# Two edits in a diffusion backbone kernel: feed-forward products added to the residual by GpSimd's transfers, and values' two parts in one stationary block

## The reference

```python
n = rmsnorm(h, norm_g[l, 0]) * (1 + sc0) + s0
h = h + 0.5 * g0 * swiglu(n, w_ffn_up[l, 0], w_ffn_down[l, 0])      # feed-forward, width 2816
n = rmsnorm(h, norm_g[l, 1]) * (1 + sc1) + s1
y, ckv, k_r = token_mix(n, ...)       # long convolution, 8-head attention, Fourier mixing, gates
h = h + g1 * y
n = rmsnorm(h, norm_g[l, 2]) * (1 + sc2) + s2
h = h + 0.5 * g2 * swiglu(n, w_ffn_up[l, 1], w_ffn_down[l, 1])
# in token_mix, per head of value width 64:
p = softmax(q @ k.T * scale);  o = p @ v
```

## Time and profile before

| | us |
|---|---|
| median of 3 runs | 3137.64 |
| the profiled execution's own time | 3137.54 |
| its span in the trace | 3135.4 |
| PE busy | 3018.9 (96%) |
| DVE busy | 2122.9 (68%) |
| ACT busy | 1141.8 (36%) |
| POOL busy | 85.8 (3%) |

### The profile page before, as it was taken

How to read it: one execution, slowest core, us unless ns; L and a number is a source line. 1 busy time by engine, 2 the same in 40 slices (tenths; PEclk the granted TensorE clock), 3 DMA queues, 4 the chain that set the end, 5 groups by cost and what they waited for, 6 DMA issues and landing times.

```text
span 3135.4 us, 48664 instructions
## 1 busy us (share of the span) xinstructions
PE 3018.9 (96%) x19892; PEld 2938.2 (94%) x19892; DVE 2122.9 (68%) x3521; ACT 1141.8 (36%) x1820; POOL 85.8 (3%) x164
## 2 busy tenths in 40 slices
PE   7999999998999999999999999999899999999998
PEld 4899999997899999999999999999789999999998
DVE  7666666646655557988968988863565556785675
ACT  3422312422444433434343433442154443443432
POOL 0000000000000000000000000000000000000000
PEclk8999999999999999999999999999999999999999
DMA  8255553345122532444322434334521242122222
GB/s 304 91 202 228 213 190 135 115 153 221 67 75 85 192 112 80 135 141 142 122 95 94 149 121 142 108 114 163 224 82 71 76 186 108 68 95 81 95 68 75
DMA packets 89743, 408.90 MB, mean 130 GB/s; under 512 B 10049, under 2 KB 13569, under 8 KB 68914
## 3 DMA queue, kind: packets, MB, share of 16 engines
q1 hardware_dynamic: 60384, 285.76, 25.6%
q0 software_dynamic: 19872, 94.53, 8.3%
q10 hardware_dynamic: 9266, 25.50, 2.2%
HBM read 359.46 MB, written 46.30 MB: 129 GB/s over the span
## 4 chain that ended last, share of the span: by engine, by line
PE 77%; DVE 14%; ACT 4%; issue 3%; DMA 1%; ACTq 0%; DVEq 0%
PE tile_psum L743 21%; PE misc_psum L860 12%; PE tile_psum L750 11%; PE misc_psum L864 6%; PE tile_psum L1215 6%; PE tile_psum L704 3%; PE tile_psum L1219 3%; PE misc_psum L669 3%; PE tile_psum L669 2%; PE tile_psum L860 2%; PE tile_psum L709 2%; PE tile_psum L1080 1%; DVE h L2254 1%; DVE wlo L2083 1%; PE tile_psum L864 1%
## 5 line engine op out<-in xcount | busy, mean ns | idle before, releaser
L743 PE MATMUL tile_psum<-n_hi,whi 128*128 128x320 f32 x1536 | 352.3, 311 | 4.0 <-issue 2.2
L743 PE MATMUL tile_psum<-n_lo,whi 128*128 128x320 f32 x1536 | 350.1, 309 | 0.0
L2083 DVE TENSOR_TENSOR wlo<-raw,whi 128x2048 fp32r<-128x2048 f32 (+4 forms) x130 | 250.6, 1930 | 114.2 <-ACT whi L1491 112.2
L743 PE MATMUL tile_psum<-x_hi,whi 128*128 128x320 f32 x1300 | 300.1, 312 | 17.4 <-DVE h L2254 11.7
L743 PE MATMUL tile_psum<-x_lo,whi 128*128 128x320 f32 x1300 | 298.3, 311 | 0.0
L743 PEld LDWEIGHTS tile_psum<-n_hi,whi 128*128 128x128 f32 x1536 | 257.6, 189 | 6.8 <-DVE n_lo L2174 4.2
L743 PEld LDWEIGHTS tile_psum<-n_lo,whi 128*128 128x128 f32 x1536 | 258.2, 189 | 0.0
L1491 ACT ACTIVATE whi<-raw 128x2048 fp32r<-128x2048 f32 (+4 forms) x130 | 208.9, 1616 | 126.7 <-DMA raw<-in_w_down 43.7
L1215 PE MATMUL tile_psum<-n_hi,whi 128*128 128x320 f32 x768 | 237.4, 320 | 11.0 <-ACT gate_out L1978 10.3
L2254 DVE SCALAR_TENSOR_TENSOR h<-tile_psum,ada_t,h 128x320 f32<-128x320 f32 (+2 forms) x408 | 154.2, 434 | 129.2 <-PE tile_psum L750 127.5
L750 PE MATMUL tile_psum<-n_hi,wlo 128*128 128x320 f32 x1536 | 241.3, 309 | 0.0
(11 more groups left out here) (384 smaller groups left out, 6450.1 us busy)
## 6 DMA issues: line engine op xcount, KB each, us to landing
w_ada<-in_w_ada POOLq DMA_DIRECT2D x72, 512.0 KB, 4.0
raw<-in_w_up SPq DMA_DIRECT2D x72, 512.0 KB, 3.8
raw<-in_w_up SPq DMA_DIRECT2D x34, 1024.0 KB, 4.9
w_ada<-in_w_ada SPq DMA_DIRECT2D x56, 512.0 KB, 6.3
raw<-in_w_gate SPq DMA_DIRECT2D x24, 1024.0 KB, 4.9
raw<-in_w_down SPq DMA_DIRECT2D x29, 768.0 KB, 4.4
whi<-table_keep SPq DMA_DIRECT2D x20, 1024.0 KB, 4.7
wlo<-table_keep SPq DMA_DIRECT2D x20, 1024.0 KB, 6.9
```

The costliest lines, as they stand in the source:

```text
L743: pe.matmul(tps[:, t.s, m, 0:TH], blk(p, m * n + k)[0], (hi, lo)[b][:, k, tok], start=k == 0 and b == 0, stop=False)
L2083: ins = dve.tensor_tensor(lo_at(r, n)[:, 0:w], raw_at(r, n)[:, 0:w], hi_at(h_, n)[:, 0:w].bitcast(F32), ALU.subtract)
```

## The change

Two edits that touch different stages.

**Down steps of the fast feed-forwards, chunks 0 to 2.** DVE's `update` is gone from them. ACT drains the slot (`stage_h`): it scales by `ada` into `hidden` (hf), two activations for j = 0 and four for j = 1, after waiting (for i > 0) until the transfer that read the same half of `hidden` in the step before has landed. POOL then issues a transfer from `hidden` to h that adds (`add_to_h`, 128 partitions x 2 x 320 elements, 320 KB), 72 in all. The `w_ada` loads stand in the same POOL program, those of step i ahead of the transfer of (i, 1). ACT waits for all transfers before it copies P5 into `hidden` in the next up phase, POOL before its next chunk, and DVE before the last down phase, which is unchanged.

**Heads.** V writes both parts of both heads into `v_parts`, 4 x 64 columns per key block: high and low of the even head, low and high of the odd one. P multiplies one block of 128 columns, high and low of its own head, by the high and by the low part of the probabilities: 10 matmuls of 512 columns and 2 of 128. The two halves of the result's rows are to be added: ACT copies the other half's 64 rows into `x_raw`, DVE adds its own 64 rows, and the slot is free. The high and low part are taken later, in a new step X of the list; for the last head that is right after P, and PE waits for it (`x_split`) before the projections.

```diff
             if n % 5 == 1:
                 order += [("P", (n - 2) // 5)]
+            elif n % 5 == 2 and n > 5:
+                order.append(("X", n // 5 - 1))
         if n % 10 == 1 and n < 5 * HEADS:
             order.append(("V", n // 10))
+    order.append(("X", HEADS - 1))
...
-        (vh, vl, krt), _ = place(SM0, ("v_hi", [P, KEYS], F32R), ("v_lo", [P, KEYS], F32R), ("q_rope_tmp", [P, TL], F32))
+        (vals2, krt), _ = place(SM0, ("v_parts", [P, KEYS // P, 4, VD], F32R), ("q_rope_tmp", [P, TL], F32))
+        v_at = [[vals2[:, :, b, :].rearrange("p (a k) v -> p a k v", a=2) for b in bs] for bs in ((0, 3), (1, 2))]
+        (xraw,), _ = place(XL, ("x_raw", [P, 8, T], F32))
...
@@ the PE program @@
+                        both = [vals2[:, kt, n % 2 * 2:n % 2 * 2 + 2, :].rearrange("p b v -> p (b v)") for kt in range(6)]
                         for kt in range(5):
-                            kk = slice((kt + 1) * P, (kt + 2) * P)
-                            mm3([tps[:, t.s, 0, :]], (vh[:, kk], vl[:, kk]), [(pth[:, kt, :], ptl[:, kt, :])], kt == 0, kt == 4)
-                        mm3([tps[:, t.s, 1, 0:TC]], (vh[:, 0:TC], vl[:, 0:TC]), [(pch[:, :], pcl[:, :])], True, True)\
-                            .then_inc(t.done, 1)
+                            for x_ in (pth, ptl):
+                                pe.matmul(tps[:, t.s, 0, :], both[kt + 1], x_[:, kt, :], start=kt == 0 and x_ is pth, stop=kt == 4 and x_ is ptl)
+                        for x_ in (pch, pcl):
+                            ins = pe.matmul(tps[:, t.s, 1, 0:TC], both[0], x_[:, :], start=x_ is pch, stop=x_ is pcl)
+                        ins.then_inc(t.done, 1)
...
                 all_read(tile_free)
+                pe.wait_ge(x_split, HEADS * (l + 1))
...
@@ the POOL program @@
+            def add_to_h(i, j):
+
+                tok = slice(j * TH, (j + 1) * TH)
+                pool.wait_ge(h_staged, due(h_staged))
+                pool.dma_start(h[:, 2 * i:2 * i + 2, tok], hf[:, :, tok], accum_op=ALU.add).then_inc(h_added[j], 16)
+                due(h_added[j], 16)
...
+                    for i in range(4):
+                        if c < 3:
+                            add_to_h(i, 0)
+                        ada_loads(plan[n + i])
+                        if c < 3:
+                            add_to_h(i, 1)
...
@@ the ACT program @@
+            def stage_h(l, section, i, j):
+
+                t = tile()
+                if i:
+                    act.wait_ge(h_added[j], due.now(h_added[j]))
+                for m in range(2):
+                    for a, b, g in HALVES[j]:
+                        ins = act.activation(hf[:, m, a:b], tps[:, t.s, m, a - j * TH:b - j * TH], ACT.Copy,
+                                             scale=ada[:, l * ADA_TILES + 8 * section + 2 * i + m, g:g + 1])
+                ins.then_inc(t.free, 1)
+                act.wait_ge(t.free, t.free_at)
+                act.sem_inc(h_staged, 1)
+                due(h_added[j], 16)
...
             def keep_p5(g):
+                if g % 6 == 0:
+                    for each in h_added:
+                        act.wait_ge(each, due.now(each))
...
                         elif j == 0 and i == 2:
                             at[0] += 6
-                            for k in range(4):
-                                fast_group(fast[0], k)
+                            fast_group(fast[0], 0)
+                        elif i == 2:
+                            fast_group(fast[0], 1)
                         if c == 0 and (i, j) in ((0, 0), (0, 1)):
                             sum_to_hi(1 if j == 0 else 3)
+                        stage_h(l, section, i, j)
+                        if (i, j) == (2, 1):
+                            fast_group(fast[0], 2)
+                        elif (i, j) == (3, 0):
+                            fast_group(fast[0], 3)
...
-                        split_hi(halves(vh[:, :]), mps[:, m.s, :, 0:KEYS // 2])
+                        for e in range(2):
+                            split_hi(v_at[0][e], v_psum(m, e))
...
-                        split_hi(xh[rows, 2 + n // 2, :], flat(tps, t.s)[rows, 0:T])
+                        other = slice((1 - n % 2) * VD, (2 - n % 2) * VD)
+                        act.activation(xraw[rows, 2 + n // 2, :], flat(tps, t.s)[other, 0:T], ACT.Copy).then_inc(x_half, 1)
+                    elif what == "X":
+                        rows = slice((n % 2) * VD, (n % 2 + 1) * VD)
+                        act.wait_ge(x_sum, due(x_sum))
+                        split_hi(xh[rows, 2 + n // 2, :], xraw[rows, 2 + n // 2, :])
...
@@ the DVE program @@
                     for i, j in walk(4):
-                        update(section, i, j)
+                        t = slots.tile()
                         if j:
                             continue
+                        if c == 0 and i == 0:
+                            seen(t)
...
-                        lo_part(halves(vl[:, :]), mps[:, m.s, :, 0:KEYS // 2], halves(vh[:, :]), m.free)
+                        dve.wait_ge(op_hi, due.now(op_hi) + 2)
+                        for e in range(2):
+                            lo_part(v_at[1][e], v_psum(m, e), v_at[0][e], (low_values, m.free)[e])
...
-                        lo_part(xl[rows, 2 + n // 2, :], flat(tps, t.s)[rows, 0:T], xh[rows, 2 + n // 2, :], t.free)
+                        dve.wait_ge(x_half, due(x_half))
+                        y = xraw[rows, 2 + n // 2, :]
+                        dve.tensor_tensor(y, y, flat(tps, t.s)[rows, 0:T], ALU.add).then_inc(t.free, 1)
+                        dve.wait_ge(t.free, t.free_at)
+                        dve.sem_inc(x_sum, 1)
+                    elif what == "X":
+                        rows = slice((n % 2) * VD, (n % 2 + 1) * VD)
+                        lo_part(xl[rows, 2 + n // 2, :], xraw[rows, 2 + n // 2, :], xh[rows, 2 + n // 2, :], x_split)
```

More of the change, by code:

```diff
@@ L1825, in _ @@
                 if l:
[L1826 removed]
+                    fast_ffn(l, 2, (l, 0), (l, 1), before_mixer)
                 else:
@@ L2481, in fast_ffn @@
                     if c == 3:
+                        for each in h_added:
+                            dve.wait_ge(each, due(each, 16 * 12))
                         return into_h_last(section, plan[n:], *last)
```

36 lines of the change are left out of this document (29 added, 7 removed).

## The result

| us | before | after |
|---|---|---|
| median of the runs (4 each) | 3137.86 | 3154.68 |
| lowest to highest | 3137.29 to 3138.24 | 3150.36 to 3160.12 |
| the profiled execution's own time | 3137.54 | 3150.36 |
| its span | 3135.4 | 3148.6 |
| PE busy | 3018.9 | 3009.8 |

The account below looks back on a forecast made before the run. PE, busy 96% of the span, was taken to bound the kernel. From 3137.54 us, -20.0 + 3.3 - 15.8 + 8 = -24.5 gave 3113 us, 0.8% faster, range 3101 to 3133.

Parts of the forecast that it names:

- Fewer matmuls, -20.0 us: Heads' P steps: 5 large and 1 small matmul fewer, 1.25 us a head, 16 heads, 20.0 us less.
- Extra passes at 0: Heads: one more ACT and DVE pass per head, and V's split, hide under PE's work and cost 0.
- My own upper bound, 16 x 1.6 + 3 = 28 us: Heads: the most that the added ACT and DVE passes and V's split could cost without cover, 28 us.
- the heads give only half: Rival: extra DVE or ACT passes hold back scores and fills in the heads; 3123 us, chance 0.12.
- x_split, +3.3 us: Before the projections: PE also waits for the last head's split, 1.65 us more in each of two layers.
- left alone: Projections: the clock's loss behind PE's wait, 16 matmuls in 4.14 us, was already there and got no term.
- Waits on L2254 gone, -15.8 us: Down steps: PE's waits for DVE's drain, 11.7 us, and slow matmuls behind them, 4.1, go if nothing replaces them.
- New waits by the adding transfers, +8 us: Chunk 0's down steps: 0.4 us at (1, 1), 1.8 at P7, up to 1.8 for the clock; 4 us in two feed-forwards.
- L: Down steps: an adding transfer's time from issue to landing, taken as 5.3 us.
- free to 5.8: Last feed-forward, which has no dots: no new wait while a transfer lands within 5.8 us.
- The slow rival: Down steps: adding transfers take about 9 us, decisive from 7.5; 3161 us, chance 0.08.
- Two of the signs named ahead: Heads' stretch shrinking under 8 us a layer would refute the prediction; PE busy falling 20 us or more would support it.

Follow-up runs that it names:

- h2_third: e3_late with a third matmul by the probabilities' low part put back into every P step; 3146.58 us against 3136.85 for the kernel before, ratio 1.0029.
- e3_late: e1_heads with step X moved from just behind P to the steps before the next head's P; 3131.60 us against 3137.93 for the kernel before.
- e1_heads: Only the heads' edit of the change, on the kernel before; 3143.92 us against 3137.93, ratio 1.0020.
- f1_copy: e2_adds with transfers that copy instead of adding; 3128.74 us against 3136.88 for the kernel before, ratio 0.9975.
- h3_act_drain: Heads' edit, X late, ready projection branch first; in chunk 0 ACT drains into `hidden`, DVE adds, no adding transfers; 3129.15 us against 3136.85 for the kernel before.
- e2_adds: Only the down steps' edit of the change, on the kernel before; 3147.03 us, ratio 1.0029.
- f2_chunk0: e2_adds in chunks 1 and 2 only, chunk 0 drained by DVE as before; 3136.82 us against 3136.88 for the kernel before, ratio 1.0003.

## Why the prediction was wrong, step by step

- **Fewer matmuls, -20.0 us.** Right as a size. 9.6 us a layer between the marks, by h2_third and e3_late, where my numbers give 9.7.
- **Extra passes at 0.** Wrong, and the largest error of the heads. The stretch of P steps of the changed kernel is as long as before (233.0 and 232.3 against 232.6 and 232.5 us): the passes ate all 9.7 us. 3.8 a layer come from the drain, V and X wherever it stands, 6.2 from X's place behind P (e1_heads against e3_late: 12.3 us for the two layers). The failing step was "16 x 0.84 = 13 us of DVE hide in heads where it is 56% busy". The share was read from a window of 250 us, but behind every P the roundings, the softmax and the values are one chain over ACT and DVE (933.97 to 946.19 us in the trace quoted). My own upper bound, 16 x 1.6 + 3 = 28 us, was nearer (20 measured). The 5.2 us of waits for the gate's drain stood in the trace and were named under the rival "the heads give only half"; that they were the end of such a chain, I did not follow.
- **x_split, +3.3 us.** The wait was right: 3.5 instead of 1.7 us, twice. The clock behind it I "left alone": 16 matmuls took 4.60 us instead of 4.14 and the next 8 took 1.59 instead of 1.17, so 0.9 a layer more. One term of the heads' edit I did not have at all: the second projection panel landed after 10.2 and 10.6 us in the two layers, before after 8.9 and 8.1, and PE waited 4.7 and 5.1 us there instead of 3.5 and 3.0.
- **Waits on L2254 gone, -15.8 us.** These waits went, but the "if nothing takes their place" did not hold even without adding: with plain copies (f1_copy) the edit gave 8.1 us, and 5.1 us of new waits stood in the three chunk 0s, 3.3 of them for a copy to land. The drain of (0, 1) was late on ACT too, since it stood behind a high part that waits for DVE, and I had cleared ACT by its busy share (11.8 of 40 us) without walking its order, though the order was shown ahead of the prediction. In the changed kernel that cost little: PE waited 0.85 us for it in each of two feed-forwards. It cost 2.1 to 3.6 us in each only where DVE adds as well (h3_act_drain). And the 10.6 us of the earlier trace rows were not nearly all in chunk 0: four of the eight waits were, 8.4 us.
- **New waits by the adding transfers, +8 us.** Wrong in size, and the failing step of the down steps' part: with the -15.8 as it stands, e2_adds' +9.1 makes this term 25 us, not 8. Adding alone costs 17 us over copying (e2_adds against f1_copy), about half of it as idle time of PE and half as longer matmuls at a lower granted clock, for which I had 1.8 us in each of two feed-forwards. Two things made L too short where it counts: "it moves twice the bytes of a copy" was the wrong picture (the trace has the same bytes in four times the packets), and I took the trace's quiet rows for the crowded places. The places of the waits were right. The transfer of (0, 1) was issued at 1259.87, behind the `w_ada` load, took 5.95 us, and PE waited 1.8 us at (1, 1) where 0.4 was computed; the one of (2, 1) took 5.96, that of (3, 1) 6.87, and PE waited 1.8 us for P1's copy behind the last drain and 1.2 for the copy behind P5's, where 1.8 was computed at P7. The last feed-forward, "free to 5.8", met 9.4 us, and PE waited 3.2 us there. I took one L for all; the steps that decide are those where SyncE loads the next chunk's panels at the same moment. (That the panels are what makes them long is read from their place in the trace; no run took the panels away.) The slow rival's L, 9 us, was there, in three transfers of chunk 0 (8.5, 9.5 and 9.4 us), and "against: every row of its size" came from rows that stood in quiet places.
- **The rival that came true** is then none alone: the slow transfers in chunk 0, with 9 us of loss instead of 40, and the heads giving nothing instead of half. Both had been priced, and the chance of both together was not. Two of the signs named ahead show it: the heads' stretch did not shrink by 8 us a layer but by nothing, and PE's busy time fell by 9 us and not by 20.
- **The Trainium skill.** Its page (DMA: Bandwidth & Descriptors, Rules for kernel authors) says that an accumulate reads its destination and writes it later. f1_copy agrees in kind: 4.0 us by adding, 2.7 by copying. The estimate of 3.5 us from its figures was 0.5 low against the shortest landing (4.0), 0.7 against the median with little beside it (4.2), and about half of the 6 to 9.4 us that decided. The hold-up of GpSimd's descriptors by VectorE (SBUF — State Buffer, Who interferes with whom) does not show: f1_copy's issues took 704 to 729 ns, all 72, with DVE busy 33.5 of 40 us in chunk 0.

The spread of the runs goes with the granted clock. The changed kernel's four runs took 3150.36, 3154.32, 3155.03 and 3160.12 us at mean clocks of 0.979, 0.977, 0.978 and 0.976; of the kernel before, beside e1_heads, the runs at 0.984 and 0.985 took 3132 to 3137 us and those at 0.981 and 0.982 took 3136 to 3142. What moves the clock from run to run remains open.

Open too is why the second projection panel lands later. It is no chance of one trace: in the ten kernels with the heads' edit 19 of 20 landings took 9.8 to 10.7 us (the other 8.8, in h2_third), in the five without it nine of ten took 8.1 to 9.3 (the other 10.2, in f2_chunk0). No experiment was made on it.

## What to carry to other kernels

A busy share says nothing about a chain: before work is added at "no cost", walk the program of its engine from the event before to the wait behind, and count what stands there in a row. A new stage's place in an in-order program is worth more than its length: X cost 6 us a layer more in one place than in another, and ACT's drain, where DVE adds behind it, gained some 5.5 us by standing one instruction earlier; where a transfer adds, the same turn changed nothing in the time. A new wait of PE can cost more than its length: beside 22 us more of idle time the changed kernel has some 11 us of matmuls that took longer, so compare busy time as well as idle time. Price a transfer where it is issued, beside what other queues start at that moment, and let the wait at the end of the chain decide, not the median.

## What the runs showed of the hardware

- An adding transfer from SBUF to SBUF of 320 KB, 128 partitions: 1.17 us to issue on POOL and 4.2 us to land (median of eight, 4.0 to 4.5) with little beside it; the same as a copy 0.71 and 2.8 (2.7 to 4.4). Beside three weight panels issued within 1 us, 9.4.
- The add goes in 256 packets of 1280 bytes, 130 ns each in the mean, the copy in 64 of 5120 bytes, 213 ns each (e2_adds and f1_copy, by their packet records).
- In a crowded stretch the adding transfers raise the DMA engines' share more than the bytes moved: 0.88 at 218 GB/s, against 0.66 at 223 with copies.
- `w_ada` loads on POOL's queue between the adding transfers took 4.8 us to land (median), where the earlier trace rows have 4.0, and their issue 531 to 1022 ns where the earlier trace rows have 527 to 539.
- Behind a wait of PE the clock sometimes fell to its lower level and sometimes not. In the changed kernel's heads, where the kernel before had 1.00 in the same windows, it was granted 0.73 from 926 to 930 us and 0.83 from 978 to 982, behind PE's waits; behind the longest wait, 2.5 us, it stayed at 1.00. The rows are 926 to 930, 946 to 950 and 978 to 982:

```profile
926.00:930.00 4.00, 4.00 (x21) 3.81 (x20) 1.19 (x5) 1.38 (x4) 0.00 (x0) 0.73 0.01 4
946.00:950.00 4.00, 3.34 (x24) 3.36 (x25) 3.61 (x10) 1.96 (x8) 0.00 (x0) 1.00 0.00 0
978.00:982.00 4.00, 4.00 (x25) 4.00 (x24) 0.82 (x1) 0.70 (x1) 0.00 (x0) 0.83 0.10 16
```

  PE is busy all of the first and the third, with 21 and 25 matmuls in 4 us.
